# Half 1's attention pieces in another order among the first expert gathers, with fewer routing pieces a pair

## What is computed

```python
h = rmsnorm(x, ln_mix_g) * (1 + sc1) + sh1
proj = h @ w_in
o_attn = nsa_mixer(q, kc, vc, ksl, vsl, kw, vw, gts, ...)   # three kinds of attention, 8 heads of 64
o_conv = short_conv_mixer(ch, cb, cc, conv_w)
mixed = concatenate([rmsnorm(o_attn) * norm_attn_g, rmsnorm(o_conv) * norm_conv_g])
x = x + gt1 * (mixed @ w_out)
h2 = rmsnorm(x, ln_ffn_g) * (1 + sc2) + sh2
x = x + gt2 * peer_ffn(h2, wq, keys, expert_u, expert_v)
```

## Time and profile before

| what | value |
|---|---|
| median of 3 runs | 1492.57 us (1492.05 to 1494.49) |
| the profiled execution's own time | 1494.17 us |
| its span, from the first to the last instruction | 1492.3 us |
| mean granted TensorE clock | 0.913 |
| busy: PE, VectorE, ScalarE, POOL | 1163.9, 766.0, 486.8, 363.1 us |
| first gather issued | 239.29 us |
| last gather issued | 955.46 us |

### The profile page before, as it was taken

How to read it: one execution, slowest core, us unless ns; L and a number is a source line. 1 busy time by engine, 2 the same in 40 slices (tenths; PEclk the granted TensorE clock), 3 DMA queues, 4 the chain that set the end, 5 groups by cost and what they waited for, 6 DMA issues and landing times.

```text
span 1492.3 us, 14830 instructions
## 1 busy us (share of the span) xinstructions
PE 1163.9 (78%) x5496; PEld 670.0 (45%) x5496; DVE 766.0 (51%) x1783; ACT 486.8 (33%) x1274; POOL 363.1 (24%) x285
## 2 busy tenths in 40 slices
PE   5899876867866776666777766679898698899896
PEld 1687644422422231111122211144776587789782
DVE  2312467868469954456444445420567765632112
ACT  1022122643333433334333233311675452211101
POOL 0677101224334423434333334200000000000000
PEclk9898787978889998998899999989999998999998
DMA  9764413779999999999999999815431221214130
GB/s 336 278 255 170 156 49 141 265 272 391 395 414 422 420 387 414 422 421 421 422 396 398 409 400 422 368 59 177 161 113 57 84 85 58 83 53 148 59 112 28
DMA packets 91875, 377.56 MB, mean 253 GB/s; under 512 B 6323, under 2 KB 9564, under 8 KB 58972
## 3 DMA queue, kind: packets, MB, share of 16 engines
q0 software_dynamic: 36864, 268.45, 44.2%
q1 hardware_dynamic: 53152, 103.98, 19.4%
q10 hardware_dynamic: 1788, 4.19, 0.9%
HBM read 375.54 MB, written 1.06 MB: 252 GB/s over the span
## 4 chain that ended last, share of the span: by engine, by line
PE 41%; DVE 25%; DMA 22%; ACT 8%; issue 3%; POOL 1%; SPq 0%; DVEq 0%; POOLq 0%; ACTq 0%
PE ps L87 41%; DMA AR<-in_puv,idx 19%; DVE AR L87 11%; DVE RT L87 3%; ACT L87 3%; DVE acc L87 3%; DMA W<-in_w_mod 2%; DVE rowb L87 2%; DVE tok L87 2%; ACT av L87 2%; ACT acc L87 1%; DVE mixT L87 1%; DVE hT L87 1%; ACT AR L87 1%; ACT rowb L87 1%
## 5 line engine op out<-in xcount | busy, mean ns | idle before, releaser
L87 PE MATMUL ps<-AR,acc 128*64 128x512 f32 x952 | 371.2, 695 | 192.5 <-ACT acc L87 190.2
L87 POOL DMA_INDIRECT AR<-in_puv,idx x256 | 271.3, 1060 | 528.6 <-PE ps L87 407.0
L87 PE MATMUL ps<-hT,W 128*128 128x256 f32 (+2 forms) x1504 | 325.0, 375 | 2.1 <-ACT hT L87 1.3
L87 PEld LDWEIGHTS ps<-hT,W 128*128 128x128 f32 (+1 forms) x1504 | 271.1, 196 | 54.1 <-issue 13.3
L87 PEld LDWEIGHTS ps<-AR,acc 128*64 128x64 f32 x952 | 89.7, 149 | 450.6 <-ACT acc L87 368.6
L87 DVE CUSTOM_DVE_ANT_0 AR<-AR,mixT 128x1024 f32<-128x1024 f32 x128 | 156.8, 1227 | 153.8 <-DMA AR<-in_puv,idx 153.6
L87 DVE CUSTOM_DVE_ANT_0 AR<-AR,tok 128x1024 f32<-128x1024 f32 x128 | 153.1, 1220 | 65.0 <-DMA AR<-in_puv,idx 64.9
L87 ACT ACTIVATE av<-av 128x1 f32<-128x1 f32 x256 | 51.2, 200 | 316.4 <-DVE av L87 315.0
L87 ACT ACT_TABLE_LOAD x103 | 132.1, 1283 | 17.1 <-issue 15.3
L87 PE MATMUL ps<-W,hT 128*128 128x512 f32 (+3 forms) x288 | 95.7, 489 | 0.0
L87 ACT ACTIVATE acc<-fold,av 128x64 f32<-128x64 f32 x238 | 82.8, 348 | 7.8
(11 more groups left out here) (223 smaller groups left out, 1103.2 us busy)
## 6 DMA issues: line engine op xcount, KB each, us to landing
W<-in_w_in SPq DMA_DIRECT2D x25, 2048.0 KB, 7.9
W<-in_w_mod SPq DMA_DIRECT2D x12, 2048.0 KB, 15.8
W<-in_w_out SPq DMA_DIRECT2D x2, 2048.0 KB, 10.2
W<-in_wq SPq DMA_DIRECT2D x2, 2048.0 KB, 12.9
AR<-in_puv,idx POOLq DMA_INDIRECT x256
W<-in_wba SPq DMA_DIRECT2D x2, 2048.0 KB, 7.6
W<-in_wbb SPq DMA_DIRECT2D x2, 2048.0 KB, 7.7
W<-in_wo SPq DMA_DIRECT2D x2, 2048.0 KB, 8.0
```

Source lines behind the costliest of these rows:

```text
L87: ins = f(*args, **kw)
```

## The change

- `attn_root(1)` squares into the first half of `junk` (as half 0 did) and takes its root into `junk[:, 512:640]`, in place of two parts of `pcA`, which lies in place 6. It waits in addition for the last add into `X` and for the norm of half 0, which used `junk`.
- The steps of `half1()` stand in another order. `q_project(0, 2)` goes from the first list to the third, `q_project(0, 3)` from the fourth to the sixth, `scores_mm(7)` from the third to the fifth, the compressed attention's steps one or two lists later, `turn_p(7)` from the sixth to the eighth, both `cmp_add` and `pv_(7)` into one list, the root from the eighth to the tenth, an empty list behind it, and the mix from the ninth to the twelfth. All that follows the mix is three pairs later.
- The diagonals go from `mixT` to `acc` after the seventh list, not after the eighth.
- Place 5 joins when `pv_(7)` is done, no longer also after the mix. Place 6 waits for the last `weigh`, the two `cmp_add` and the routing's last use of the scratch, no longer for `pv_(7)` and the mix. They join the ring at the same pairs as before.
- For p below 12 the routing is advanced by 4 pieces a pair, not by 8.

```diff
@@ -708,13 +708,14 @@
                 t_mix[a].append(V(stt, mixT[:, 4 + j, c], oc[:, j, c], PV[:, V_NC + j:V_NC + j + 1], n, MUL, MUL,
                                   after=[e, t_oc[a][j]] + t_mc))
 
-        osqs = (osq0, pcA[:, 0:512].rearrange("p (j t) -> p j t", j=4))
-        rats = (nrm[:, 2, :], pcA[:, 512:640])
+        osqs = (osq0, osq0)
+        rats = (nrm[:, 2, :], junk[:, 512:640])
         t_os = {}
 
         def attn_root(a):
             t = A(act, osqs[a], O[a].t[:, :].rearrange("p (j t) -> p j t", j=4), ACT.Square,
-                  after=[stage[3 + 4 * a, "O"], stage[1 + 4 * a, "O"]] + t_g1 + t_c["o", 0] + t_c["o", 1])
+                  after=[stage[3 + 4 * a, "O"], stage[1 + 4 * a, "O"]] + t_g1 + t_c["o", 0] + t_c["o", 1] + t_jx[-1:]
+                  + ([t_n[0]] if a else []))
             t_os[a] = t
             norm_root(("a", a), rats[a], osqs[a], [t])
 
@@ -1051,23 +1052,26 @@
 
         def half1():
 
-            yield [lambda: weigh(5), lambda: q_project(0, 2), lambda: scores_mm(6)]
-            yield [lambda: scores_add(6), lambda: turn_p(5), lambda: cmp_s1(1)]
-            yield [lambda: cmp_s2(1), lambda: weigh(6), lambda: pv_(5), lambda: scores_mm(7)]
-            yield [lambda: cmp_s3(1), lambda: scores_add(7), lambda: turn_p(6), lambda: q_project(0, 3)]
+            yield [lambda: weigh(5), lambda: scores_mm(6)]
+            yield [lambda: scores_add(6), lambda: turn_p(5)]
+            yield [lambda: weigh(6), lambda: pv_(5), lambda: q_project(0, 2)]
+            yield [lambda: turn_p(6), lambda: cmp_s1(1)]
             t_keys[1] = SP.dma(nc.sync.dma_start, s_k, kT_sb[1], keys3, after=[stage[6, "T"]])
-            yield [lambda: weigh(7), lambda: pv_(6), lambda: cmp_turn(1, 0)]
-            yield [lambda: turn_p(7), lambda: cmp_turn(1, 1)]
-            load_row(0, [stage[7, "T"]])
-            yield [lambda: pv_(7)]
-            yield [lambda: cmp_add(1, 0), lambda: cmp_add(1, 1), lambda: attn_root(1)]
+            yield [lambda: cmp_s2(1), lambda: pv_(6), lambda: scores_mm(7)]
+            yield [lambda: cmp_s3(1), lambda: scores_add(7), lambda: q_project(0, 3)]
+            yield [lambda: weigh(7), lambda: cmp_turn(1, 0), lambda: cmp_turn(1, 1)]
             late_t["dg"] = stage[7, "e"]
             t_dgs = [t for f in dg_free for t in f]
-            yield [lambda: attn_mix(1, t_dgs)]
             t_eq["hold"] = [late_t["dg"]]
             eqbuf[0] = acc[:, 1, :].rearrange("p (h s j) -> p h s j", h=4, s=16)
-            ring.append([5, [stage[7, "O"], t_mix[1][-1]]])
-            late_t["six"] = [stage[7, "O"], t_mix[1][-1]]
+            yield [lambda: turn_p(7)]
+            load_row(0, [stage[7, "T"]])
+            yield [lambda: pv_(7), lambda: cmp_add(1, 0), lambda: cmp_add(1, 1)]
+            late_t["six"] = [stage[7, "e"]] + t_c["o", 0] + t_c["o", 1]
+            ring.append([5, [stage[7, "O"]]])
+            yield [lambda: attn_root(1)]
+            yield []
+            yield [lambda: attn_mix(1, t_dgs)]
             yield [lambda: attn_mm(1, 0, 0, 4)]
             yield [lambda: attn_mm(1, 0, 4, 8)]
             yield [lambda: attn_mm(1, 1, 0, 4), lambda: attn_add(1, 0)]
@@ -1212,7 +1216,7 @@
                 for f in todo_:
                     f()
                 break
-            advance(routes[0], 8)
+            advance(routes[0], 4 if p < 12 else 8)
             if "six" in late_t and not t_eq["open"]:
                 ring.append([6, late_t.pop("six") + [t_eq["last"]]])
             if (0, 7) in t_gw and len(routes) == 1 and len(t_qp[1]) == 4:
```

## The result

The changed kernel takes 1482.88 us (median of 4 runs, 1481.87 to 1485.62), the kernel before 1493.53 us beside it (4 runs, 1492.05 to 1495.51). The ratio is 0.9926, with a 95% interval of 0.9909 to 0.9943: 10.65 us faster. The forecast was 1476.4 us in a range from 1469.5 to 1486.0. The way it moved and the place were as forecast, and the time lies in the range; the gain was forecast 5.5 us too large.

The account below looks back on a forecast made before the run. Bound: bytes over DMA rate, behind 100 us (240 to 340) with 28.8 us of idle DMA. Sum: -18.2 (early ring) + 2.0 (returned work) = -16.2 us from the 1492.57 us median, so 1476.4 us; range 1469.5 to 1486.

Parts of the forecast that it names:

- What bounds the kernel: DMA stands idle for 28.8 us between 240 and 340 us; only what shortens that can pay.
- Order: Early pairs: unit 6's scores no longer stand behind the projection, some 3.8 us; the mix's 5.9 us wait goes.
- What is late next is the ring itself: Early pairs, once those waits go: the ring of five sets the pace, above VectorE's 4.9 us a pair.
- Pace of the ring of five: Pairs 0 to 11: 6.5 us a pair, so pair 12 starts at 329.8 in place of 347.99, 18.2 us earlier.
- The landing: A gather in the early ring: 8.12 us to land, about 0.8 of it waiting behind the gather before it.
- The returned work: Pairs 12 to 24: 20.3 us of VectorE work comes back, chiefly into idle time; 2 us allowed as loss.
- At nothing: Places 5 and 6: their changed waits cost nothing, as both were free before POOL reached them.
- Rival 1: Pairs 12 to 21: returned VectorE work starves DMA, 8 us come back; gain 10.2, 1482.4 us; chance 0.17.
- Rival 2: Early ring: a gather lands in 6.5 us with an empty line, pace 5.9; 1470.2 to 1472.2 us; chance 0.18.
- Rival 3: Early pairs: PSUM banks make PE steps wait ahead of a pair's products; pace 9.0 us, 1504.4 us; chance 0.04.
- rival 4: Before 340 us: idle DMA is only moved, as weight loads would have used it; no change; chance 0.05.
- The tell-tales: Changed profile: pair 12 near 330, DMA share near 0.88 from 240 to 330, then 1.0; 16 us earlier from pair 50.

Follow-up runs that it names:

- both edits: Changed kernel with attention's PE steps ahead of the pair's own and both query projections cut in halves: 1479.48 us with 4 routing pieces, 1478.64 with 8.
- e4_late: Changed kernel with places 5 and 6 joining the ring only after the mix, two pairs later: 1485.42 us, 0.9954 of the kernel before.
- e5_early: Changed kernel with a pair's attention steps on PE and the root recorded ahead of its gelu and products: 1485.34 us, 0.9946 of the kernel before.
- e6_early_split: e5_early with the two query projections of half 0 also cut in halves: 1479.48 us, 0.9911 of the kernel before.
- e3_split: Changed kernel with the two query projections of half 0 cut in halves over two pairs each: 1481.74 us, 0.9921 of the kernel before.

## Why the prediction was right, and where its size was off

1. *What bounds the kernel.* Right. The gain was made where DMA stood idle, between 240 and 340 us, and most of it (11.6 of 12.4 us at pair 12) was still there at pair 53. The work that leaves VectorE was about right too: between the first dots of pairs 0 and 12 it was busy for 75.1 us before and 57.7 now, 17.4 less, for a forecast of 79 to 59 us, 20.3 less.
2. *Order.* Right that it is the larger part (9.5 us alone), and that the mix's wait goes: the reciprocal starts without a wait and the mix right behind it, at 333.57. Wrong by leaving out where the moved steps landed. I priced the projection only in front of unit 6's scores, where it left; at its new place it holds pair 3's gelu on ScalarE by 5.6 us. "What is late next is the ring itself" is the sentence that failed: late next was what stands ahead of the gelu on ScalarE: the projection's copy in pair 3, and in pair 7 the compressed attention's copy and the routing's exponential with its two table loads.
3. *Pace of the ring of five.* 6.5 us forecast, 6.9 measured: 78.0 us for twelve pairs and 83.0. These 5.0 us, and 0.8 by which pair 0 starts later, are the whole difference between 18.2 and 12.4. The nearness is partly luck, for two errors cancel. The landing was taken as 8.12 us and is 5.5 with an empty line: by that the ring alone would run at (5.5 + 1.2 + 0.95 + 3.2)/2 = 5.4 us a pair. The other 1.5 us a pair, 18 us in twelve pairs, are waits that the sum didn't hold. The halves took away 2.1 of the 18; products at the lower clock (4.47 for 1.94 us) are another part. Most of the 18, some 15 us, isn't split up by the runs. The Trainium skill, DMA: Bandwidth & Descriptors, section "Anatomy of one DMA", gives 2.0 us plus bytes over 436 GB/s, an estimate of 4.4 us for this transfer; the trace's 5.5, which runs to the start of the dot, is 1.1 above it. The row that I preferred was 2.6 above the measurement. It held more than the wait of 0.8 that I took out for the gather issued 4.84 us ahead. The issue on POOL took 1.84 us, where 0.94 is usual, and at 301.59, 1.6 us behind it, SP issued a load of 512 KB (`rowb<-in_rows`); 0.49 MB of SP's queue moved between 304 and 309 us. In the changed kernel gather 23 stands 4.79 us behind the one before it, without such a load, and its dot, for which VectorE waits, starts 5.9 us after the issue (325.53 to 331.44). So the gather ahead explains little of the 2.9 us between 8.42 and 5.5; the load and the long issue are the likely cause, which no run takes apart.
4. *The returned work.* 2 us allowed. With the changed kernel's order 2.5 were measured between pairs 12 and 53, with the old order none, with both edits about 6. It isn't a constant: it depends on what else is late in pairs 12 to 24. VectorE's work came back where forecast.
5. *At nothing:* places 5 and 6. Right for this change. The two pairs of delay that it keeps off are worth 2.5 to 4 us (`e4_late`). The token of place 6 is later than needed, which costs nothing at the ring's tail (gather 28, which takes place 6, goes out at 335.07 with no idle time but 0.30 us) and 8 us at its head.
6. *The rivals.* Rival 1 named 1482.4 us, next to the measured 1482.88, but by another mechanism: it has pair 12 at 330 and loses 8 us behind it, and the loss lies ahead of pair 12. Rival 2's landing (6.5 us) was, if anything, too slow, and still its gain didn't come, since the ring wasn't the only thing. Rival 3 (banks, pace 9.0) didn't occur: between 252 and 336 us PE waited for VectorE once, for 0.3 us. Nor did rival 4.
7. *The tell-tales.* Pair 12 at 335.6, between the forecast 330 and the 340 that would have refuted it; DMA at 1.02 and 1.01 from 340 to 540, above the 0.97 asked for. The share of 240 to 330 was to be 0.88 and is 0.75: I had put all the idle time left, 10.6 us, there, and it is 23 us. From pair 50 on all was to be 16 us earlier: pair 50 is 10.0 earlier (564.57 against 574.59). Idle share and gain in time don't go one for one: 240 to 340 moved 299 GB/s in the mean now and 266 before, which is 3.3 MB or 3.1 gathers, 7.8 us at 2.48 us each (an estimate from these rows, which takes the weight loads to be alike). The other 3.8 us of the 11.6 at pair 53 fit the rate behind 340, 412 and 417 against 403 and 410 GB/s, which I had taken as full: 1.6 MB more in 200 us, 1.5 gathers. What sets that 2% wasn't found.

## What to carry to other kernels

Where engines run their queues in order, a step that is moved has to be priced at the place where it lands as well: read there, for each engine that it touches, what now stands behind its wait. Merely swapping a long step with its neighbour moved the wait and made the kernel slower (`e5_early`); cut into halves (3.84 us into two of 2.05) the same order was 5.9 us faster (`e6_early_split`; the intervals just touch), while the halves alone gained 2.1 us in the trace's early pairs and nothing that the medians can tell. Before buffers are taken in a new order, look whether the token they wait for is their own last reader's. A latency that is taken from a row in a busy stretch holds whatever else the DMA engines moved meanwhile, other queues' loads too. And positions in a trace are compared from a common event, here pair 0, since its start alone scattered by 3.3 us.

## What was not expected of the hardware

A gather of 1.05 MB in 128 rows has its dot start 5.5 us after its issue with an empty line, where 8.42 were seen beside another queue's load of 512 KB. Eight products of 64x512 take 1.94 us at a granted clock of 1.00 (`e3_split`, 276.30 to 278.30 us) and 4.47 at 0.51 (310.20 to 314.80), after PE had been idle for 4.48 us: such a wait for PE's input was paid twice. And the DMA rate in stretches with a busy share of 1.01 to 1.02 ranged from 403 to 417 GB/s.
